# Hybrid decoder layer on one core: four more gate panels computed as block-product pairs ahead of the attention, four fewer threaded through it

## The chip, the cores and the metric

The kernel runs on one core of one Trainium2 chip. The metric is the device time of one execution in microseconds; the median of three runs is compared. The profile is of a fourth execution.

## The reference

One decoder layer on 512 tokens of width 2048, all in float32. Cut to what matters here:

```python
h = rmsnorm(x, norm_mix_g)                      # 512 x 2048
proj = h @ w_in                                 # q, six k/v streams, branch gates, u, v, merge gates
q, kv, nsa_g, u, v, merge_g = split(proj)       # merge_g: 2 x 2048 columns
kc, vc = compress_blocks(kv[0]), compress_blocks(kv[1])
o_a = nsa_attention(q, kc, vc, kv[2], kv[3], kv[4], kv[5], sigmoid(nsa_g))
o_b = spatial_gating(gelu(u), gelu(v), ...)
g = sigmoid(merge_g)                            # 512 x 2 x 2048
merged = g[0] * (o_a @ w_proj_a) + g[1] * (o_b @ w_proj_b)
x = x + merged @ w_mix_out
x = x + cross_attention(rmsnorm(x), rmsnorm(mem))
x = x + (silu(gt) * up) @ w_ffn_out             # gt, up = rmsnorm(x) @ w_ffn_in
out = rmsnorm(x)
```

The attention has 16 heads in 4 groups of keys, dimension 64, and for each query three softmaxes: over 31 compressed tokens, over selected blocks of 64 (all eight of them are selected here, so this one is plain causal attention) and over a window of 512.

## The kernel before

**Products.** Every float32 operand is split into a high and a low part; a product of 128 x 128 weights with 512 tokens is three TensorE matmuls of 512 columns (high with high, high with low, low with high; lines 987 to 989). The program calls the weight block with its three matmuls a *tile*. A *panel* is 128 output columns of a projection: 16 tiles, whose weights come in four *quarters*. For each quarter ScalarE casts the raw weights to the high part (`high`, line 2210) and VectorE subtracts to get the low part (`low`, line 1519, or both in `split`, lines 1498 and 1500). These two operations are called a split below.

**Block-product pairs.** Two panels can instead be made as a *pair*: the product of the 2 x 2 blocks (two weight halves by two halves of the inner dimension and of the tokens) by seven instead of eight block products, each a `half_unit` (lines 1078 to 1090) of 8 steps with 512 + 256 columns each. `G_TILES` lists which panels are made so: keys and values to compress, values, queries, and ten of the merge gates. Each pair costs ScalarE seven casts of 128 x 1024 and three evacuations, VectorE seven subtractions and some sums, SP three loads, GpSimd one adding DMA, and ScalarE two stores to HBM (`g_store`). Three buffers for the split weights are used in turn (`wg_hi`, `wg_lo`, unit number modulo 3); two of the three share their memory with the split buffers of plain panels (`w_hi`, `w_lo`).

**The order of stages** before the attention: memory keys and values; six plain merge-gate panels ("m0", `PLAIN_GATES`); the pairs (`G_PAIRS` of them); two key projections, value rows, the compression; then the attention; then the spatial gate ("sv", "su"), and the projections "ab", where all 32 gate panels are read back from HBM.

**The attention** is written out by hand as a list of *steps*, run by all engines in their own order. Its work is 32 *halves* (numbers `hu` 0 to 31): for each of four query chunks `qi` of 128 queries (first chunk to fourth chunk: 128, 256, 384, 512 keys), four key groups, and two pairs of heads. A half takes two score steps in the first chunk, four in the second and third, five in the fourth. Per step:

- TensorE (`scores`, line 1188) makes scores; VectorE (line 1714) masks them and takes maxima; ScalarE (line 2427) makes exponentials and their sums.
- After the last score step of a half, s, VectorE makes coefficients (1 over the sums, times the branch gate; lines 1726 and 1730) in step s+1, right after the maxima of that step. GpSimd scales the half's probabilities by them: first the compressed block for both heads (line 2798), then four blocks of 128 queries by 128 to 512 keys (line 2803).
- TensorE turns (transposes) the scaled probabilities: in step s+2 the compressed ones (line 1201), from step s+3 on the others, two 128-key blocks of both heads per step (line 1204). In the first chunk the first such turning needs all four of GpSimd's blocks, in the others two. ScalarE and VectorE split the result (lines 2445, 1742), and two steps after the turning TensorE weighs the values with it (`weigh`, lines 1215, 1219; `LAG = 2`). The last turning of a half falls into the first score step of the next or the one after, and in all but the first chunk the turning in step s is one of the half before.

```python
if part == 0 and 0 < hu <= len(HALVES):        # VectorE, in step s + 1, after low_max(step)
    dve.wait_ge(exp_done, step)
    dve.reciprocal(coef[:, ub], den[:, ub])
```

**What is threaded through it.** The merge-gate panels that are neither plain nor in pairs are computed between the attention's own matmuls. `spread` (line 170) deals their tiles to the 129 steps so that each step gets about the same TensorE cost, by `step_cost`; in a step, TensorE takes a third of the tiles ahead of the scores, a third ahead of the turning, and the rest ahead of the weighing. Where a step ends a quarter, ScalarE and VectorE split a later one at the end of that step, three quarters ahead, VectorE after its other work and so before the maxima of the next step; where it ends a panel, ScalarE evacuates and stores the gates (`gates_out`, line 2290).

```python
for step in range(STEPS):                      # TensorE
    tiles = TILES_AT[step]
    third = (len(tiles) + 2) // 3
    gate_tiles(tiles[:third])
    ...
    scores(step)
    gate_tiles(tiles[third:2 * third])
    ...
    turn_probs(*TURN_AT[step])
    gate_tiles(tiles[2 * third:])
```

## Time and profile before

| what | us |
|---|---|
| median of 3 runs | 2755.34 (2754.51 to 2755.74) |
| the profiled execution | 2756.18 |
| its span, first to last instruction | 2754.4 |
| its mean granted TensorE clock | 0.998 |
| stage of the 13 pairs | 143.2 to 398.5 |
| attention, first scores to first row of the spatial gate | 472.0 to 792.9 |

The profile is one execution of the program. The engines are PE (TensorE's matmuls), PEld (its weight loads, which overlap the matmuls), DVE (VectorE), ACT (ScalarE), POOL (GpSimd) and SP. L12 is line 12 of the kernel. A time in brackets behind a row is how long the engine was idle before it, and what ended that. A matmul's end is modelled, so distances are read from start to start.

### The profile page before, as it was taken

Reading aid. Unit: us, or ns where it says so; the run is one execution under the profiler, and the core shown is the slowest. Engines: PE = TensorE matmul, PEld = TensorE weight load, DVE = VectorE, ACT = ScalarE, POOL = GpSimd, SP = SyncE. Lnnn points to the kernel's source line nnn. Section 1 sums busy time; section 2 is a strip of 40 time slices with the busy share of each in tenths; the row PEclk is TensorE's granted clock in tenths of the full one; section 3 lists DMA queues with packets and bytes.
Section 4 is the critical chain, followed back from the end, with each engine's and each line's share of the span. In section 5 each row is a group of like instructions: output and inputs, shape, how many; then the busy total and the mean of one; then the engine's idle time right before and its main releaser. Section 6 shows DMA issues by size and latency. Waiting matters only on the chain.

```text
span 2754.4 us, 38103 instructions
## 1 busy us (share of the span) xinstructions
PE 2713.5 (99%) x14221; PEld 2301.5 (84%) x14221; DVE 2105.2 (76%) x2998; ACT 1209.7 (44%) x1923; POOL 450.5 (16%) x418
## 2 busy tenths in 40 slices
PE   8999999999999999999999999999999999999997
PEld 7888888888888888888877888888888888888886
DVE  6777874667755555555687899999999998988887
ACT  6344432766631222211144555555555555443334
POOL 0000002545520545411000000000000000010000
PEclk9999999999999999999999999999999999999999
DMA  8488866332233455444345788888888888999982
GB/s 243 131 188 181 199 157 165 81 92 66 58 96 99 105 141 152 137 115 114 92 137 142 165 214 205 218 204 210 204 214 211 210 206 250 301 305 297 302 263 92
DMA packets 648106, 479.38 MB, mean 174 GB/s; under 512 B 14612, under 2 KB 589448, under 8 KB 642056
## 3 DMA queue, kind: packets, MB, share of 16 engines
q1 hardware_dynamic: 568048, 416.58, 51.6%
q0 software_dynamic: 58896, 36.70, 10.2%
q10 hardware_dynamic: 21000, 23.92, 2.7%
q8 instruction: 103, 1.69, 0.3%
q14 instruction: 59, 0.48, 0.1%
HBM read 413.98 MB, written 63.18 MB: 173 GB/s over the span
## 4 chain that ended last, share of the span: by engine, by line
PE 89%; DVE 5%; ACT 3%; issue 2%; POOL 1%; DMA 1%; DVEq 0%; ACTq 0%; SPq 0%
PE banks L987 10%; PE banks L988 10%; PE banks L989 10%; PE banks L1419 10%; PE banks L1416 9%; PE banks L1417 9%; PE banks L1481 4%; PE banks L1483 4%; PE banks L1482 4%; PE banks L1085 3%; PE banks L1088 3%; PE banks L1086 3%; PE banks L1188 1%; PE banks L1204 1%; PE banks L1247 1%
## 5 line engine op out<-in xcount | busy, mean ns | idle before, releaser
L987 PE MATMUL banks<-act_hl,w_hi 128*128 128x512 f32 (+1 forms) x816 | 325.8, 399 | 2.4 <-DVE w_lo L1519 2.4
L1498 DVE CAST w_hi<-raw 128x512 fp32r<-128x512 f32 (+1 forms) x232 | 139.8, 603 | 245.0 <-PE banks L989 166.7
L988 PE MATMUL banks<-act_hl,w_hi 128*128 128x512 f32 (+1 forms) x816 | 319.7, 392 | 0.0
L989 PE MATMUL banks<-act_hl,w_lo 128*128 128x512 f32 (+1 forms) x816 | 319.5, 392 | 0.0
L1417 PEld LDWEIGHTS banks<-t_hl,wf_lo 128*128 128x128 f32 x1312 | 246.5, 188 | 58.3
L1419 PE MATMUL banks<-t_hl,wf_hi 128*128 128x512 f32 x656 | 259.4, 396 | 0.0
L1416 PE MATMUL banks<-t_hl,wf_hi 128*128 128x512 f32 x656 | 259.2, 395 | 0.0
L1417 PE MATMUL banks<-t_hl,wf_lo 128*128 128x256 f32 x1312 | 257.7, 278 | 0.0
L1951 DVE TENSOR_TENSOR wf_lo<-raw_f,wf_hi 128x1024 fp32r<-128x1024 f32 x164 | 200.4, 1222 | 56.7 <-ACT wf_hi L2599 56.7
L2599 ACT ACTIVATE wf_hi<-raw_f 128x1024 fp32r<-128x1024 f32 x164 | 173.8, 1060 | 136.9 <-PE banks L1419 83.6
L1417 PEld LDWEIGHTS banks<-tok_hl,wf_lo 128*128 128x128 f32 x984 | 184.8, 188 | 43.7
L1481 PE MATMUL banks<-wo_hi,h_full 128*128 128x512 f32 x560 | 218.9, 391 | 0.8 <-DVE wo_lo L1985 0.8
L1483 PE MATMUL banks<-wo_lo,h_full 128*128 128x512 f32 x560 | 218.0, 389 | 0.0
L1482 PE MATMUL banks<-wo_hi,h_full 128*128 128x512 f32 x560 | 217.9, 389 | 0.0
L1419 PE MATMUL banks<-tok_hl,wf_hi 128*128 128x512 f32 x492 | 194.6, 396 | 0.0
L1416 PE MATMUL banks<-tok_hl,wf_hi 128*128 128x512 f32 x492 | 194.4, 395 | 0.0
L1417 PE MATMUL banks<-tok_hl,wf_lo 128*128 128x256 f32 x984 | 193.3, 278 | 0.0
L2599 ACT ACTIVATE wf_hi<-s 128x1024 fp32r<-128x1024 f32 x123 | 130.2, 1059 | 137.9 <-PE banks L1419 137.9
L1500 DVE TENSOR_TENSOR w_lo<-raw,w_hi 128x512 fp32r<-128x512 f32 (+1 forms) x232 | 180.8, 779 | 8.0
L989 PEld LDWEIGHTS banks<-act_hl,w_lo 128*128 128x128 f32 (+1 forms) x816 | 152.5, 187 | 34.4
L2889 POOL DMA_DIRECT2D s<-in_w_ffn_in_dram x40 | 62.1, 1554 | 705.6 <-DMA s<-in_w_ffn_in_dram 705.6
L987 PEld LDWEIGHTS banks<-act_hl,w_hi 128*128 128x128 f32 (+1 forms) x816 | 152.8, 187 | 28.1 <-issue 3.0
(357 smaller groups left out, 6568.8 us busy)
## 6 DMA issues: line engine op xcount, KB each, us to landing
raw_f<-in_w_ffn_in_dram SPq DMA_DIRECT2D x82, 1024.0 KB, 9.0
raw<-in_w_in_dram SPq DMA_DIRECT2D x42, 1024.0 KB, 5.6
h_full<-hidden_blocks SPq DMA_DIRECT2D x35, 1024.0 KB, 8.1
wo_raw<-in_w_ffn_out_dram SPq DMA_DIRECT2D x32, 1024.0 KB, 10.0
raw_g<-in_w_in_dram SPq DMA_DIRECT2D x26, 1024.0 KB, 8.8
hidden_blocks<-tok_hl SPq DMA_DIRECT2D x44, 512.0 KB, 6.1
s<-in_w_ffn_in_dram SPq DMA_DIRECT2D x40, 512.0 KB, 6.2
s<-in_w_ffn_in_dram POOLq DMA_DIRECT2D x40, 512.0 KB, 6.5
```

Source lines behind the costliest of these rows:

```text
L987: pe.matmul(dst, w_hi[:, q, j, 0:m], hi, start=first, stop=False)
L988: pe.matmul(dst, w_hi[:, q, j, 0:m], lo, start=False, stop=False)
L989: return pe.matmul(dst, w_lo[:, q, j, 0:m], hi, start=False, stop=last)
L1416: pe.matmul(dst, w_h[:, k], both(k), start=start and k == 0, stop=False, skip_group_check=True)
L1417: mm = pe.matmul(dst[:, 0], w_l[:, k], both(k)[:, 0], start=False, stop=False, skip_group_check=True)
L1419: mm = pe.matmul(dst, w_h[:, k], both(k), start=False, stop=last, skip_group_check=True)
L1481: pe.matmul(dst, hi, wo_hi[g % 3][:, k], start=STARTS[j] and q == 0 and k == 0, stop=False, skip_group_check=True)
L1482: pe.matmul(dst, lo, wo_hi[g % 3][:, k], start=False, stop=False, skip_group_check=True)
L1483: mm = pe.matmul(dst, hi, wo_lo[g % 3][:, k], start=False, stop=last, skip_group_check=True)
L1500: dve.tensor_tensor(w_lo[:, q, :, 0:width], src, w_hi[:, q, :, 0:width].bitcast(F32), ALU.subtract).then_inc(split_done, 1)
L1951: dve.tensor_tensor(wf_lo[g % 3][:].rearrange("p k n -> p (k n)"), src, wf_hi[g % 3][:].rearrange("p k n -> p (k n)").bitcast(F32), ALU.su ...
L2599: act.activation(wf_hi[g % 3][:].rearrange("p k n -> p (k n)"), src, ACT.Copy).then_inc(f_hi, 1)
```

## The change

Four merge-gate panels (numbers 16 to 19) go from the attention to the list of pairs: 15 pairs in place of 13, 12 threaded panels (192 tiles) in place of 16 (256 tiles). The number of half units becomes 105 in place of 91, and the last one falls on another of the three buffers; the first two entries of the two buffer lists are exchanged for that, and with them a wait in ScalarE's order: the cast for unit 0 now writes where the last plain gate panel's first two quarters lie, and comes after the wait for them. The `LAG` of two steps between turning and weighing is the same in both.

```diff
--- before.py
+++ after.py
@@ -38,9 +38,9 @@
 PAIRS = FK - PLAIN
 HK, HT = DK // 2, T // 2
 PLAIN_GATES = 6
-G_TILES = [("c", n) for n in range(0, 4, 2)] + [("v", n) for n in range(0, 4, 2)] + [("q", n) for n in range(0, 8, 2)] + [("merge", n) for n in range(PLAIN_GATES, PLAIN_GATES + 10, 2)]
+G_TILES = [("c", n) for n in range(0, 4, 2)] + [("v", n) for n in range(0, 4, 2)] + [("q", n) for n in range(0, 8, 2)] + [("merge", n) for n in range(PLAIN_GATES, PLAIN_GATES + 14, 2)]
 G_PAIRS = len(G_TILES)
-GATES_AHEAD = PLAIN_GATES + 10
+GATES_AHEAD = PLAIN_GATES + 14
 OUT_H = (2, 4, 4, 4, 4, 4)
 OUT_M0 = (0, 2, 6, 10, 14, 18)
 OUT_RUNS = [(c, b) for c in range(len(OUT_H)) for b in range(2)]
@@ -58,7 +58,7 @@
 
 
 
-assert G_PAIRS % 2 == 1 and (7 * G_PAIRS - 1) % 3 == 0
+assert G_PAIRS % 2 == 1 and (7 * G_PAIRS - 1) % 3 == 2
 assert 2 * sum(OUT_H) == FK and PAIRS % 2 == 1 and T // 64 <= 16 and T <= 512
 
 
@@ -256,8 +256,8 @@
 
         gate_m0 = at("gate_m0", [P, 2, T], F32, C + 32 * KIB)
         raw_g = [at("raw_g0", [P, 2, 2, HK * P], F32, C), at("raw_g1", [P, 2, 2, HK * P], F32, base)]
-        wg_hi = [at(f"wg_hi{i}", [P, HK, P], F32R, o) for i, o in enumerate((C + 24 * KIB, base + 16 * KIB, base + 20 * KIB))]
-        wg_lo = [at(f"wg_lo{i}", [P, HK, P], F32R, o) for i, o in enumerate((C + 28 * KIB, base + 24 * KIB, base + 28 * KIB))]
+        wg_hi = [at(f"wg_hi{i}", [P, HK, P], F32R, o) for i, o in enumerate((base + 16 * KIB, C + 24 * KIB, base + 20 * KIB))]
+        wg_lo = [at(f"wg_lo{i}", [P, HK, P], F32R, o) for i, o in enumerate((base + 24 * KIB, C + 28 * KIB, base + 28 * KIB))]
         n_hl = [at(f"n_hl{k}", [P, 2, 4 * HT], F32R, B + 8 * k * KIB) for k in range(HK)]
         n_hi, n_lo = ([n_hl[k][:, w].rearrange("p (a t) -> p a t", t=HT) for k in range(HK)] for w in range(2))
         n_sum = [at(f"n_sum{k}", [P, 4, HT], F32, B + (8 * k + 4) * KIB) for k in range(HK)]
@@ -2314,8 +2314,8 @@
                     row_sums_high(k - 1)
                 if q == 1:
                     gates_out(ph, n - 1, n - 1, gate_m0)
+            act.wait_ge(quarters_done, ph.end() - 2)
             g_unit_high(0)
-            act.wait_ge(quarters_done, ph.end() - 2)
             g_unit_high(1)
             gates_out(ph, ph.n - 1, ph.n - 1, gate_m0)
             def g_store(p):
```

`spread` deals the 192 tiles anew over all 129 steps, so the tiles move in every part of the attention. Three places, each as the engine's list has it, before and with the change. In the names, prob and prob_c are the probabilities that GpSimd scales, act_hl is the split normalised input and w_hi, w_lo the split gate weights, so three rows L987, L988, L989 are one gate tile.

TensorE, half 29 (fourth chunk), from the turning of the compressed probabilities to the first turning of the others, before:

```order
L1201 MATMUL banks<-ident,prob_c 32x128 x2
L1219 MATMUL banks<-prob_t_111,v_hl 128x256 x4
L987 MATMUL banks<-act_hl,w_hi 128x512
L988 MATMUL banks<-act_hl,w_hi 128x512
L989 MATMUL banks<-act_hl,w_lo 128x512
L1188 MATMUL banks<-k_sel,q_hl 128x512 x2
L1204 MATMUL banks<-ident,prob 128x128 x4
```

and with the change:

```order
L1201 MATMUL banks<-ident,prob_c 32x128 x2
L1219 MATMUL banks<-prob_t_109,v_hl 128x256 x4
L1188 MATMUL banks<-k_sel,q_hl 128x512 x2
L1204 MATMUL banks<-ident,prob 128x128 x4
L1219 MATMUL banks<-prob_t_110,v_hl 128x256 x4
```

One tile that stood between the two turnings is gone from there.

TensorE, half 21 (third chunk), from the turning in the first score step after s to the turning of the compressed probabilities, before:

```order
L1204 MATMUL banks<-ident,prob 128x128 x4
L1219 MATMUL banks<-prob_t_109,v_hl 128x256 x4
L987 MATMUL banks<-act_hl,w_hi 128x512
L988 MATMUL banks<-act_hl,w_hi 128x512
L989 MATMUL banks<-act_hl,w_lo 128x512
L1188 MATMUL banks<-k_sel,q_hl 128x416 x2
L987 MATMUL banks<-act_hl,w_hi 128x512
L988 MATMUL banks<-act_hl,w_hi 128x512
L989 MATMUL banks<-act_hl,w_lo 128x512
L1201 MATMUL banks<-ident,prob_c 32x128 x2
```

and with the change:

```order
L1204 MATMUL banks<-ident,prob 128x128 x4
L1219 MATMUL banks<-prob_t_109,v_hl 128x256 x4
L987 MATMUL banks<-act_hl,w_hi 128x512
L988 MATMUL banks<-act_hl,w_hi 128x512
L989 MATMUL banks<-act_hl,w_lo 128x512
L1188 MATMUL banks<-k_sel,q_hl 128x416 x2
L1201 MATMUL banks<-ident,prob_c 32x128 x2
```

One of two tiles is gone here; a second one is gone ahead of the first of these turnings.

VectorE, half 21, from the split of the turned probabilities in step s to the coefficients in step s+1, before:

```order
L1742 TENSOR_TENSOR prob_t_110<-banks,prob_t_110 128x512
L1749 TENSOR_TENSOR oa<-banks,o_low 64x128 x2
L1519 TENSOR_TENSOR w_lo<-raw,w_hi 128x512
L1714 ISA banks,attn_max<-banks,cmp_mask 128x32
L1714 ISA attn_max 128x1
L1714 ISA banks,attn_max<-banks,causal 128x384
L1714 ISA attn_max 128x1
L1726 RECIPROCAL coef<-den 128x6
```

and with the change:

```order
L1742 TENSOR_TENSOR prob_t_110<-banks,prob_t_110 128x512
L1749 TENSOR_TENSOR oa<-banks,o_low 64x128 x2
L1714 ISA banks,attn_max<-banks,cmp_mask 128x32
L1714 ISA attn_max 128x1
L1714 ISA banks,attn_max<-banks,causal 128x384
L1714 ISA attn_max 128x1
L1726 RECIPROCAL coef<-den 128x6
```

The low part of a gate quarter (L1519) is gone from the end of this step; it stands in another.

## Rows read from the trace of the kernel before

**Rows 1.** The page, first part: busy time, share of the span, instructions.

```profile
PE 2713.5 (99%) x14221; PEld 2301.5 (84%) x14221; DVE 2105.2 (76%) x2998; ACT 1209.7 (44%) x1923; POOL 450.5 (16%) x418
```

**Rows 2.** Stretches: pairs, attention. Length, busy by engine, clock, DMA share, GB/s.

```profile
143.20:398.50 255.30, 254.38 (x1459) 221.52 (x1458) 199.89 (x206) 116.30 (x131) 18.68 (x12) 1.00 0.77 176
...
472.00:792.90 320.90, 315.48 (x1827) 265.48 (x1826) 215.45 (x719) 213.66 (x641) 161.60 (x193) 1.00 0.27 74
```

**Rows 3.** Waits of the attention: waiter, releaser, total us, times, longest.

```profile
POOL prob_c L2798 <- DVE coef L1730: 144.5, 32, 7.1
...
PEld banks L1204 <- POOL prob L2803: 9.5, 20, 1.0
...
PE banks L1204 <- POOL prob L2803: 2.9, 5, 0.8
```

**Rows 4.** Chain that ended last, plain panel: third matmul of 14 successive tiles.

```profile
460.30 0.24 PE banks L989
...
469.49 0.24 PE banks L989
```

**Rows 5.** Groups of instructions in the attention: count, busy us, mean ns, idle before.

```profile
L1519 DVE TENSOR_TENSOR w_lo<-raw,w_hi 128x512 fp32r<-128x512 f32 x63 | 45.9, 729 | 50.7 <-ACT w_hi L2210 50.2
L2210 ACT ACTIVATE w_hi<-raw 128x512 fp32r<-128x512 f32 x63 | 39.2, 623 | 0.0
```

**Rows 6.** Chain that ended last, start of the pairs: a cast, a subtraction.

```profile
147.57 1.07 ACT wg_hi L2307
148.66 1.24 DVE wg_lo L1599
```

**Rows 7.** Timeline, half 29: turning at s, GpSimd's scaling, first needed turning.

```profile
745.71 0.60 PE L1204 MATMUL banks<-ident,prob 128*128 128x128 f32 x4
...
748.60 0.70 POOL L2798 TENSOR_SCALAR prob_c<-prob_c,coef 128x32 f32<-128x32 f32 x2 [5.21 <-DVE coef L1730]
749.27 6.20 POOL L2803 TENSOR_SCALAR prob<-prob,coef 128x512 f32<-128x512 f32 x4
...
752.44 0.66 PE L1204 MATMUL banks<-ident,prob 128*128 128x128 f32 x4
```

**Rows 8.** Timeline, the same of halves 19 and 21.

```profile
631.75 0.60 PE L1204 MATMUL banks<-ident,prob 128*128 128x128 f32 x4
...
635.30 0.70 POOL L2798 TENSOR_SCALAR prob_c<-prob_c,coef 128x32 f32<-128x32 f32 x2 [4.12 <-DVE coef L1730]
...
638.49 0.66 PE L1204 MATMUL banks<-ident,prob 128*128 128x128 f32 x4
...
651.33 0.60 PE L1204 MATMUL banks<-ident,prob 128*128 128x128 f32 x4
...
655.53 0.70 POOL L2798 TENSOR_SCALAR prob_c<-prob_c,coef 128x32 f32<-128x32 f32 x2 [4.76 <-DVE coef L1730]
...
658.72 0.66 PE L1204 MATMUL banks<-ident,prob 128*128 128x128 f32 x4 [0.54 <-POOL prob L2803]
```

**Rows 9.** Chain that ended last, inside half 21's interval.

```profile
653.82 0.69 DVE w_lo L1519
```

**Rows 10.** Timeline, half 13: turning at s, GpSimd's blocks, first needed turning.

```profile
571.66 0.60 PE L1204 MATMUL banks<-ident,prob 128*128 128x128 f32 x4
...
576.33 3.70 POOL L2803 TENSOR_SCALAR prob<-prob,coef 128x256 f32<-128x256 f32 x4
...
578.91 0.60 PE L1204 MATMUL banks<-ident,prob 128*128 128x128 f32 x4
```

**Rows 11.** Timeline, half 3: GpSimd's blocks, weight load of the needed turning.

```profile
497.34 2.35 POOL L2803 TENSOR_SCALAR prob<-prob,coef 128x128 f32<-128x128 f32 x4
...
499.74 0.31 PEld L1204 LDWEIGHTS banks<-ident,prob 128*128 128x128 f32 x3 [0.52 <-POOL prob L2803]
```

**Rows 12.** Timeline, half 27: turning at s, first needed turning.

```profile
720.87 0.60 PE L1204 MATMUL banks<-ident,prob 128*128 128x128 f32 x4
...
728.29 0.66 PE L1204 MATMUL banks<-ident,prob 128*128 128x128 f32 x4
```

## The prediction

> **What bounds the kernel now.** I read the page's first part, then a table of stretches, then the waits of the attention, then its timeline half by half. The page has TensorE busy 99% of the span [rows 1]. The stretches show where that share is an average: the stage of 13 block-product pairs (143.2 to 398.5 us) has VectorE at 78% and GpSimd nearly empty, the attention stretch (472.0 to 792.9 us) has 320.9 us with TensorE at 315.5, VectorE at 215, ScalarE at 214 and GpSimd at 162 us [rows 2]. So both stages look bound by TensorE. The waits of the attention say how close the second one is to something else: TensorE's matmuls wait 2.9 us in 5 places for GpSimd's scaled probabilities (L2803), its weight loads 9.5 us in 20 places for the same line; GpSimd itself waits 144.5 us in 32 places, once per half, for VectorE's coefficients [rows 3]. That is the sign of a chain that is only just covered, once in each of 32 halves. What covers it is the gate work between its ends, and this is what the change takes out.
>
> **The two prices.** A gate tile (three 512-column matmuls) takes 0.707 us: 13 tiles lie between the two starts 460.30 and 469.49 [rows 4]. A whole panel of 16 tiles is 11.3 us. A pair of block products gives two panels in 254.4 us / 13 = 19.6 us [rows 2].
>
> **What the change adds and removes.** Four panels leave the attention: 64 x 0.707 = 45.2 us of TensorE work. Two more pairs come ahead of it: 2 x 19.6 = 39.1 us. On TensorE alone: **6.1 us less**. In the pair stage VectorE is busy 15.4 us of each 19.6 and ScalarE 8.9, and the DMA share is 0.77 [rows 2], in a steady rhythm, so two more pairs should cost what the 13 cost, their loads, stores and GpSimd's adding DMAs included. In the attention 16 splits leave ScalarE (0.62 us each, L2210) and VectorE (0.73 us each, L1519), four gate evacuations and stores leave ScalarE, and SP has four panel loads less [rows 5]; none of these engines ends the stage by its sum, but the splits matter below.
>
> **The swapped buffers and the moved wait.** The first unit's weights now go to the place that the last plain gate panel's first two quarters hold, so ScalarE's first cast waits until TensorE has two quarters left. Those are 24 matmuls, 8 x 0.707 = 5.7 us. Behind the wait stand one cast (1.07 us) and one VectorE subtraction (1.24 us) before unit 0 can start [rows 6], 2.3 us, so I cost it at nothing; the second cast stands where it stood. Uncovered it would cost at most 2.3 us. The third unit goes on waiting for the last gate store, as now.
>
> **The chain in each half.** Call s the last score step of a half. TensorE turns probabilities of the half before in step s; ScalarE copies them out, VectorE subtracts, adds the closed half, sometimes splits a weight quarter, takes the maxima of step s+1, and only then makes the coefficients; GpSimd scales the small block and then two (for the first query chunk four) probability blocks; only then can TensorE turn them, in step s+3. I call the time from the turning in s to the one in s+3 the interval. It cannot be shorter than the chain, and not shorter than TensorE's own work in it.
> - Fourth chunk (512 keys, half 29): turning 745.71, GpSimd starts 748.60, first needed turning 752.44, an interval of 6.73 us with 2.89 + 3.84, the latter being 0.67 plus half of 6.20 [rows 7]. Four tiles lie in it, and TensorE stands there as soon as GpSimd is done: the cover is just used up. Half 30 reads the same, 28 too.
> - Third chunk (384 keys): half 19 has no split at s: 3.55 + 3.19 = 6.74 us, no matmul waits; half 21 has one: 4.20 + 3.19 = 7.39 us, and TensorE has waited 0.54 us there [rows 8]. In the chain of half 21 the split's 0.69 us stands right ahead of the maxima [rows 9]. Five tiles lie in each.
> - Second chunk (256 keys, half 13): interval 7.25 us with 7 tiles and no wait; GpSimd starts its four blocks at 576.33 and has the two that are needed ready 1.85 us later, at 578.2; TensorE comes at 578.91 [rows 10]: 0.7 us to spare with a split in the chain, and more in halves without one.
> - First chunk (128 keys, half 3): GpSimd ends at 497.34 + 2.35 = 499.69 and TensorE's weight load starts at 499.74, having waited 0.52 us [rows 11]. Nothing to spare in most halves.
>
> **The sum.** The order now places fewer tiles in each interval. The planner gives, before and after, counted in the listed order:
> - fourth chunk: 6,5,5,5,4,4,4,6 tiles become 4,3,3,3,3,3,3,5. The four last halves lose one tile each with nothing to spare: 4 x 0.7 = 2.8 us of new waiting. The first four lose two (1.4 us), but their chain, 7.42 us in half 27 [rows 12] with ScalarE and VectorE busier there, may fall towards 6.7; I take 1.0 us each. Together 6.8 us.
> - third chunk: TensorE's own work is 6.7 us with 5 tiles, so 3.2 without any. The counts 7,5,5,5,5,5,5,5 become 4,3,4,4,3,3,3,3: work of 6.0 us in three halves and 5.3 in five. The chain is 6.74 us, or 7.4 where a split stays at s (halves 17, 20 and 23). Waiting: 3 x 2.1 + 3 x 0.75 + 2 x 1.45 = 11.5 us, against 5 x 0.7 in the halves that have a split at s now and about 1 us in the three others, 4.5 us. Together 7.0 us more.
> - second chunk: mostly two tiles less (1.4 us) against 0.7 us or more to spare, and splits that move to other halves: 2.5 us.
> - first chunk: one tile less per half, 8 x 0.7 = 5.7 us at most, its intervals overlap; I take about half, 2.5 us.
>
> New waiting 18.8 us, saved work 6.1 us: **+12.7 us**. The profiled execution took 2756.2 us (span 2754.4); that makes 2768.9 in its terms, and the median of the runs is 0.8 us lower: **2768 us**.
>
> Bounds: if every tile taken from the third and fourth chunk's intervals is lost (27 x 0.707 = 19.1 us), all of the first chunk's (5.7) and 5 us of the second's, the change costs 29.8 - 6.1 = 24 us. If the chains shorten all the way, because VectorE and ScalarE have a quarter fewer splits, and only the four last halves and those without a split wait, some 6 us come against 6.1 saved: no change.
>
> **A rule weighed against this.** The stretch table has TensorE busy 98% of the attention, more than any other engine [rows 2]. The Trainium skill (Perfetto Trace Analysis, Identifying the Most-Contended Engine) says the engine with the highest occupancy is the one to optimise first; by that rule alone the result would be 6.1 us less. The busy row agrees with it, the 20 waits do not. The same page (Optimization Strategy) says that a kernel with stretches of different contended engines may gain from interleaving them; that rule speaks against moving gate work out of the attention, and by it the result is above the old time, as in my sum.
>
> **The rivals.**
> - *TensorE stays the bound* (the chains shorten as fast as the work): 2755.3 - 6.1 = 2749 us. For it: TensorE's matmuls wait for GpSimd only 2.9 us of 320.9 now [rows 3], and VectorE has a third of the stretch free. Against it: the 20 waits of the weight loads, and half 29, whose chain holds no split that could leave it.
> - *Cover and saving cancel*: new waiting of 1 to 11 us, 2750 to 2760 us. For it: the spare time of the second chunk and the shorter queue ahead of each coefficient.
> - *The attention is bound by the other engines throughout*: it keeps its 320.9 us, and the two pairs come on top: 2755.3 + 39.1 = 2794 us. Against it: the little waiting now, and the second chunk's time to spare.
> - *The clock*: granted TensorE clock is 1.00 (2.4 GHz) in the attention in spite of its waits [rows 2]; longer waits could lower it. I give this no price, 1 in 50 inside the upper cases.
>
> **The numbers.** A measurement of this kernel tells about 0.2% (5.5 us) from no change: faster is below 2749.8, slower above 2760.8. My forecast, 2761 to 2778 us, has 0.74; cancelling 0.16; TensorE still the bound 0.06; wholly bound by others, or above 2778 for another reason, 0.04. The range leaves out the fastest case and the last one: 2753 to 2778 us.
>
> **What would show it.** Right: the pair stage 39 us longer; the attention stretch about 26 us shorter, not 45; TensorE waiting for L2803 in most of 32 places, for a total near 20 us; in half 29 three tiles and an interval still of 6.7 us; granted clock 1.00. Wrong: an interval that shrinks with its tiles (the chain then had spare time in the queues of ScalarE and VectorE), or waits that name L1519, L2290 or a DMA in place of GpSimd, or a pair that costs other than 19.6 us.

## The result and the profile after

The changed kernel takes 2779.8 us (median of four runs, 2778.81 to 2780.18), the kernel before 2755.54 us (2754.51 to 2756.91) beside it: a ratio of 1.0087 with a 95% interval of 1.0070 to 1.0105. It is **24.3 us slower**. The prediction was 2768 us, 2753 to 2778 us: the right side, about half the size, and the result lies 1.8 us above the range. The profiled execution took 2779.68 us, its span 2778.0 us.

The first part of the page, to be read beside [rows 1]:

```profile
PE 2711.4 (98%) x14253; PEld 2297.3 (83%) x14253; DVE 2124.0 (76%) x3014; ACT 1215.7 (44%) x1923; POOL 453.8 (16%) x420
```

TensorE does 2.1 us less work in a span that is 23.6 us longer. The whole loss is idle time on the engine that was taken to be the bound. The page does not say where; the stretches do. Pairs and attention of the changed kernel (length, busy time by engine, clock, DMA share, GB/s), to be read beside [rows 2]:

```profile
141.60:435.50 293.90, 293.02 (x1681) 255.24 (x1680) 230.75 (x238) 134.31 (x151) 21.76 (x14) 1.00 0.78 177
510.40:815.20 304.80, 274.88 (x1633) 228.20 (x1631) 203.79 (x702) 200.86 (x621) 160.49 (x193) 1.00 0.22 60
```

With the ends taken at the same instructions in both kernels (start of the first to start of the last matmul of the pairs, first score of the attention to the first row of the spatial gate; the rows above begin up to 0.5 us earlier):

| us | before | after | difference | predicted |
|---|---|---|---|---|
| pairs | 254.8 | 293.7 | +38.9 | +39.1 |
| attention | 320.4 | 304.7 | -15.7 | -26.4 |
| all the rest | 2179.2 | 2179.5 | +0.3 | 0 |

The pairs cost what 2 x 19.6 us said. The rest moves between 2178.5 and 2182.5 us over all the kernels of this study, so its 0.3 us is not the change's. What is left is the attention: 45.2 us of tiles left it and it became only 15.7 us shorter, so **29.5 us of new waiting** came, where 18.8 us were forecast. In the changed kernel TensorE is busy 274.9 of 304.8 us there, against 315.5 of 320.9 us before.

The waits of the attention, changed kernel (waiter, releaser, total us, times, longest), to be read beside [rows 3]:

```profile
POOL prob_c L2798 <- DVE coef L1730: 132.0, 32, 6.1
...
PEld banks L1204 <- POOL prob L2803: 27.0, 27, 2.2
PEld banks L1201 <- POOL prob_c L2798: 19.3, 24, 1.9
PE banks L1204 <- POOL prob L2803: 18.7, 22, 1.7
...
PE banks L1201 <- POOL prob_c L2798: 10.3, 13, 1.6
```

L2803 makes TensorE's matmuls wait in 22 places for 18.7 us, nearly the predicted "total near 20 us", though not "in most of 32 places". But a second line stands beside it: the turning of the small block (L1201) waits for GpSimd's scaling of that block (L2798) for 10.3 us in 13 places, where it had waited 0.7 us in 2 places. GpSimd scales that block first, as soon as it has the coefficients. A wait there says that the coefficients themselves are late, not that GpSimd is slow. The prediction had only L2803 in view. The same row in the kernel before:

```profile
PE banks L1201 <- POOL prob_c L2798: 0.7, 2, 0.6
```

By query chunk (128, 256, 384 and 512 keys, eight halves each). Windows of the kernel before:

```profile
472.00:519.90 47.90, 46.59 (x275) 38.62 (x274) 31.55 (x158) 37.23 (x143) 26.09 (x49) 1.00 0.25 67
519.90:598.30 78.40, 77.80 (x444) 66.40 (x443) 51.44 (x185) 51.81 (x164) 34.34 (x48) 1.00 0.36 96
598.30:679.10 80.80, 78.40 (x454) 65.63 (x452) 57.18 (x181) 55.21 (x160) 43.41 (x48) 1.00 0.29 78
679.10:776.60 97.50, 97.07 (x573) 81.76 (x573) 68.99 (x185) 63.08 (x164) 54.77 (x49) 1.00 0.19 55
```

and of the changed kernel:

```profile
510.40:555.40 45.00, 40.01 (x246) 33.29 (x244) 31.12 (x160) 35.06 (x140) 25.94 (x49) 1.00 0.24 65
555.40:629.10 73.70, 68.32 (x395) 57.09 (x396) 48.34 (x179) 49.34 (x159) 33.48 (x47) 1.00 0.31 83
629.10:706.00 76.90, 68.29 (x405) 56.37 (x403) 54.32 (x177) 52.01 (x154) 43.42 (x49) 1.00 0.21 55
706.00:800.90 94.90, 84.66 (x512) 70.02 (x512) 64.39 (x180) 59.13 (x158) 54.59 (x49) 1.00 0.14 42
```

Tiles taken out of each (counted in the order) at 0.707 us, less what the chunk shrank by (measured from the first score at 472.5 and 510.5 us), is its new waiting:

| chunk | tiles out | their work | shrank by | new waiting | predicted |
|---|---|---|---|---|---|
| first | 9 | 6.4 | 2.5 | 3.9 | 2.5 |
| second | 16 | 11.3 | 4.7 | 6.6 | 2.5 |
| third | 16 | 11.3 | 3.8 | 7.5 | 7.0 |
| fourth | 20 | 14.1 | 2.6 | 11.5 | 6.8 |

(The last three tiles lie behind the fourth chunk and waited 0.1 us.) The third chunk is right, the fourth and the second carry the miss: 4.7 and 4.1 us of 10.7.

### The profile page after: what moved, and what is told of

Same layout as the page of the kernel before. It is cut to its first block, busy times and chain, and to the rows that moved or that the text cites. A ratio compares the mean times of both kernels' runs of the same rounds, so it can differ in the third digit from the quotient of the medians.

```text
span 2778.0 us, 38195 instructions
## 1 busy us (share of the span) xinstructions
PE 2711.4 (98%) x14253; PEld 2297.3 (83%) x14253; DVE 2124.0 (76%) x3014; ACT 1215.7 (44%) x1923; POOL 453.8 (16%) x420
## 4 chain that ended last, share of the span: by engine, by line
PE 81%; DVE 7%; POOL 4%; ACT 3%; issue 2%; DMA 2%; ACTq 0%; DVEq 0%; POOLq 0%; SPq 0%
PE banks L1419 9%; PE banks L1416 9%; PE banks L1417 9%; PE banks L987 8%; PE banks L989 8%; PE banks L988 8%; PE banks L1481 4%; PE banks L1482 4%; PE banks L1483 4%; PE banks L1085 3%; PE banks L1088 3%; PE banks L1086 3%; POOL prob L2803 2%; DVE w_lo L1519 1%; PE banks L1247 1%
## 5 line engine op out<-in xcount | busy, mean ns | idle before, releaser
L987 PE MATMUL banks<-act_hl,w_hi 128*128 128x512 f32 (+1 forms) x752 | 299.4, 398 | 3.0 <-DVE w_lo L1519 2.4
L989 PE MATMUL banks<-act_hl,w_lo 128*128 128x512 f32 (+1 forms) x752 | 293.8, 391 | 0.0
L988 PE MATMUL banks<-act_hl,w_hi 128*128 128x512 f32 (+1 forms) x752 | 293.8, 391 | 0.0
L989 PEld LDWEIGHTS banks<-act_hl,w_lo 128*128 128x128 f32 (+1 forms) x752 | 140.1, 186 | 31.6
L987 PEld LDWEIGHTS banks<-act_hl,w_hi 128*128 128x128 f32 (+1 forms) x752 | 140.4, 187 | 27.0 <-issue 3.6
## 6 DMA issues: line engine op xcount, KB each, us to landing
wo_raw<-in_w_ffn_out_dram SPq DMA_DIRECT2D x32, 1024.0 KB, 10.5
```

What stands on the lines that cost most here:

```text
L987: pe.matmul(dst, w_hi[:, q, j, 0:m], hi, start=first, stop=False)
L988: pe.matmul(dst, w_hi[:, q, j, 0:m], lo, start=False, stop=False)
L989: return pe.matmul(dst, w_lo[:, q, j, 0:m], hi, start=False, stop=last)
```

## What the longer chain consists of

Half 28, in the fourth chunk, with the changed kernel. TensorE's timeline (start, busy us, line; the bracket is idle time ahead of it):

```profile
757.26 0.60 PE L1204 MATMUL banks<-ident,prob 128*128 128x128 f32 x4
...
758.16 0.60 PE L1204 MATMUL banks<-ident,prob 128*128 128x128 f32 x4
...
766.27 0.44 PE L1204 MATMUL banks<-ident,prob 128*128 128x128 f32 x2 [1.72 <-POOL prob L2803]
```

The turning in step s is the one at 758.16, the first needed one in step s+3 the one at 766.27: an interval of 8.11 us, where the prediction had 6.7 us. There is another turning, that of step s-1, at 757.26, only 0.90 us ahead of it. No gate tile stands between the two any more; in half 29 of the kernel before two of them and a score stood there, and the two turnings lay 2.29 us apart.

The chain that ended last goes through that earlier turning (start, length, engine, line). In this view a matmul begins where the one before it is let go, so its starts lie a little behind those of the timeline:

```profile
757.42 0.45 PE banks L1204 x4
...
757.89 0.61 ACT prob_t L2445
...
758.52 0.69 DVE prob_t L1742
759.22 0.19 DVE oa L1749
...
759.44 0.28 DVE oa L1749
...
759.75 0.69 DVE w_lo L1519
760.45 0.61 DVE banks L1714
...
761.11 0.55 DVE prob_t L1742
761.66 0.10 DVE banks L1714
...
761.97 0.19 DVE coef L1726
...
762.18 0.17 DVE coef L1730
...
762.44 0.70 POOL prob_c L2798 x2
763.14 3.09 POOL prob L2803 x2
```

From 758.52 to 762.35 us VectorE is in the chain without a break. It works off one step (subtraction L1742 for the turning of s-1, two closing adds L1749, the gate split L1519), the maxima L1714 of step s, the subtraction for the turning of s, the maxima of s+1, and then the coefficients. The turning in s is late for none of it: its own result is only wanted at 761.11 us. **In this half the chain starts at the turning in s-1**, and from there to GpSimd's start it is 762.44 - 757.26 = 5.18 us.

The same distance stood in the trace of before, in a row that the prediction did not ask for. TensorE's timeline of the kernel before, the turning in s-1 of half 29:

```profile
743.42 0.60 PE L1204 MATMUL banks<-ident,prob 128*128 128x128 f32 x4
```

GpSimd starts at 748.60 [rows 7]: 5.18 us again. In the halves 26 to 31 of the kernel before it is 5.18 or 5.19 us every time, while the distance from the turning in s is 3.58 us in two of them and 2.89 or 2.90 in four. All measured in the two timelines, in us:

| half | before: s-1 to GpSimd | s to GpSimd | after: s-1 to GpSimd | s to GpSimd |
|---|---|---|---|---|
| 26 | 5.18 | 3.58 | 5.64 | 4.04 |
| 27 | 5.19 | 3.59 | 5.86 | 4.27 |
| 28 | 5.18 | 2.89 | 5.18 | 4.28 |
| 29 | 5.18 | 2.89 | 4.51 | 2.92 |
| 30 | 5.18 | 2.90 | 5.19 | 3.60 |
| 31 | 5.18 | 2.89 | 5.01 | 3.41 |

In the changed kernel neither distance is constant. Halves 24, 28 and 30 have 5.18 or 5.19 us with a split in step s-1, and half 29 has 4.51 us without one. In halves 26, 27 and 31 the chain that ended last also passes through ScalarE's queue: its exponentials, in half 27 the cast of a split behind them, and in half 26 the evacuation of a gate panel, which stands ahead of the copy of the turning in s:

```profile
734.71 0.50 ACT gate_out L2290
```

So it is the queues of VectorE and ScalarE from step s-1 on that make the coefficients late, and only in the fourth chunk. In the third, the turning in s-1 lies 2.4 to 3.0 us ahead of that in s, and in half 21 the chain that ended last begins at the turning in s, in both kernels. There it is the distance from s that repeats, as predicted: 3.55 us in halves 19 and 20 before and 18, 21 and 22 after, all without a split in step s, and 4.20 or 4.21 us with one in halves 17, 21 and 22 before and 20 after.

From GpSimd's start to the first needed turning it is 3.83 us in all the halves of the table. That makes a loop in the fourth chunk of the kernel before: from one first needed turning, 3.06 us of TensorE's own work to the turning in s-1, 5.18 us to GpSimd's start, 3.83 us to the next first needed turning, 12.07 us in all. The kernel before starts GpSimd every 12.06 to 12.08 us from half 25 to half 31. In the changed kernel the seven steps from half 24 to half 31 (714.26 to 797.10 us) take 11.83 us each on the mean, in spite of two or three tiles (1.4 to 2.1 us) less per half: only the 3.06 us can shrink (to 2.36 us where a tile is gone there), and what stands between s-1 and s+3 is ScalarE's, VectorE's and GpSimd's.

## The experiments

Each row is a time in the same measurement as the kernel before; where a row names no number of runs it is a single one, good to about 2 us (the runs of the kernel before in these measurements gave 2754.5 to 2758.3 us). Gains over the changed kernel are taken from its 2779.8 us.

| kernel | us | before beside it | attention |
|---|---|---|---|
| e1: before, wait moved alone | 2756.6 | 2756.4 | 320.2 |
| e2: before, twelve panels threaded, 13 pairs | 2741.9 | 2756.4 | 305.6 |
| e3: after, coefficients before maxima | 2776.2 | 2756.4 | 300.7 |
| e4: before, the same | 2754.8 | 2756.4 | 319.7 |
| e5: after, gate splits a step later | 2766.9 | 2757.0 | 292.1 |
| e6: after, everything late | 2766.9 | 2757.0 | 288.9 |
| e7: after, other places for the tiles | 2773.3 | 2757.0 | 297.7 |
| e8: before, everything late | 2751.5 | 2757.0 | 315.9 |
| e9: after, GpSimd in smaller pieces | 2777.3 | 2756.0 | 301.2 |
| e10: after, combined | 2753.4 (10 runs) | 2756.0 | 278.2 |
| e11: before, combined | 2746.5 (5 runs) | 2756.0 | 310.5 |
| e12: after, combined, other places | 2750.1 (10 runs) | 2755.3 | 275.5 |

The column on the attention is the steadiest measure, since the stages outside it and the pairs, whose code is the same, add up to 2178.5 to 2182.5 us.

### e1: the moved wait alone

```diff
-            g_unit_high(0)
             act.wait_ge(quarters_done, ph.end() - 2)
+            g_unit_high(0)
             g_unit_high(1)
```

> The kernel before, with ScalarE's wait for the last plain panel's quarters moved ahead of the first unit's cast, and nothing else. If the moved wait is covered: 2755.5 us, within 1 us, the first unit starting as before. If it is a part of the loss: up to 2.3 us more (2757.8).

2756.57 us against 2756.38 us. The chain that ended last at the start of the pairs, to be read beside [rows 6]:

```profile
146.86 1.07 ACT wg_hi L2307
...
147.96 1.24 DVE wg_lo L1599
```

The cast and the subtraction stand in the chain as they did before, and the wait cost nothing. The pair stage, the other edit outside the attention, is measured above as +38.9 us.

### e2: twelve panels threaded, without the pairs

This kernel leaves out the four panels that the change moves: they are not computed, and one DMA fills their rows from the input.

```diff
-GATES_AHEAD = PLAIN_GATES + 10
+GATES_AHEAD = PLAIN_GATES + 14
```

> The kernel before with 12 threaded gate panels in place of 16 and still 13 pairs; four gate panels are not computed (their rows are filled from x by one DMA in the attention). If the whole loss beyond the pairs' price lies in the attention's own waits: the attention stretch falls from 320.9 to about 305 us as with the full change, and the time is 2755.5 - 16 = 2739.5 us (2738 to 2742). If some of the loss comes from the two added pairs or from the swapped buffers, the attention shrinks by more than 20 us and the time is below 2736.

2741.92 us, and the stretch of the attention (columns as above):

```profile
472.70:778.30 305.60, 276.11 (x1630) 229.53 (x1629) 203.83 (x702) 200.77 (x621) 160.23 (x193) 0.99 0.23 64
```

305.6 us, as in the changed kernel (304.7); the second to fourth chunk are each within 0.1 us of its, and the first is 1.0 us longer. So the lost time belongs to the attention with twelve panels in it. It is not brought on by what the two pairs leave behind, their DMAs or their buffers. Against the kernel before beside it e2 gains 14.5 us, where the changed kernel loses 24.3: 38.8 us for the two pairs.

### e3 and e4: coefficients ahead of the maxima

The first theory, which took the chain from the turning in s: VectorE's coefficients stand behind the maxima of step s+1, so put them first. e3 is the changed kernel, e4 the one before.

```diff
             for step in range(STEPS):
                 hu, part = STEP_OF[step] if step < ITEMS else (len(HALVES), step - ITEMS)
-                if step < ITEMS:
-                    low_max(step)
                 if part == 0 and 0 < hu <= len(HALVES):
...
                     dve.tensor_tensor(coef[:, ub], coef[:, ub], gates[:, qi, j * 12 + 6 * pr:j * 12 + 6 * pr + 6], ALU.mult).then_inc(coef_done, 1)
+                if step < ITEMS:
+                    low_max(step)
```

> The changed kernel, with VectorE making the coefficients of a closed half ahead of the maxima of step s+1 in place of behind them. Theory A (the chain runs through VectorE's queue, and the maxima of step s+1 and TensorE's scores stand in it for nothing): GpSimd starts 0.5 to 1.1 us sooner in most of the 32 halves, TensorE's waiting for GpSimd falls from 29 to 5 to 12 us, the time to 2757 to 2764 us. Rival B (the coefficients wait for the exponentials of step s anyway, or GpSimd's own blocks bound it): under 5 us gained, 2775 to 2780. Rival C (the later maxima delay the exponentials by as much): no gain, or slower.

> The kernel before with the same exchange on VectorE. Theory A: TensorE's matmuls wait only 3.6 us for GpSimd in it, its weight loads some more; 2 to 4 us gained, 2751.5 to 2753.5. Rivals B and C: 2755.5 or more.

e3 gave 2776.15 us, a gain of 3.6 us where 16 us or more were expected: a miss, inside what rival B gave. e4 gave 1.6 us where 2 to 4 were expected, which a single run does not tell from nothing; its attention is 0.7 us shorter. Waits of the attention in e3:

```profile
PE banks L1204 <- POOL prob L2803: 16.0, 20, 1.7
...
PE banks L1201 <- POOL prob_c L2798: 5.5, 9, 1.1
```

and VectorE's timeline in half 28 of e3:

```profile
758.75 0.19 DVE L1724 RECIPROCAL coef<-den 128x6 f32<-128x6 f32 x1 [0.30 <-ACT prob L2427]
```

The coefficients now wait for ScalarE's exponentials of step s, and those wait for VectorE's maxima of s, which stand behind the gate split and the closing adds of the step before. In the third chunk the distance from the turning in s to GpSimd fell (halves 21 and 22: 3.55 to 2.98 us). In the fourth it did not: half 28 has 5.19 us from s-1 and 4.29 us from s, as without the edit. By chunk the attention changed by +0.2, -1.0, -2.8 and -0.4 us: a gain in the third, where the chain starts at s, and next to none in the fourth. There, what held the coefficients up was not what stands behind the turning in s, and this run turned the theory to s-1.

### e5: the gate splits one step later

If VectorE's queue from s-1 on is the chain, then taking a gate split out of it must shorten it, wherever the turning in s lies. The edit runs the splits of a step after the next step's maxima and coefficients. Nothing is left out. A split of step s thus goes behind the coefficients, but one of step s-1 only goes behind the maxima of s, and stays ahead of them.

```diff
+                if step:
+                    gate_lows(step - 1)
                 short = len(SCORES[min(hu, len(HALVES) - 1)]) == 2
...
-                for k in QUARTERS_AT[step]:
-                    k += AHEAD
...
+            gate_lows(STEPS - 1)
```

> The changed kernel, with VectorE's part of each gate split (L1519) moved from the end of its step to behind the maxima and coefficients of the next. Theory A2 (VectorE's queue from the turning in step s-1 to the coefficients is the chain; a split in it costs 0.7 us, and one stands in it in about half of the 32 halves, at step s-1 or s): 8 to 12 us gained, 2768 to 2772 us, and half 28's time from the turning in s to GpSimd falls from 4.3 to about 3.6 us. Rival D (GpSimd and ScalarE hold the chain, VectorE only follows): under 3 us gained.

2766.91 us, 12.9 us less than the changed kernel and 1.1 us below what was expected of the s-1 theory. The attention lost 12.6 us. From s-1 to GpSimd's start it is 4.48 to 5.01 us in the fourth chunk, where it was 4.51 to 5.86.

One expectation was missed, and it tells most: in half 28 the distance from the turning in s was to fall to 3.6 us and came out at 4.11. Its split is one of step s-1, and it is still in the chain that ended last, now between the maxima of s and the subtraction for the turning in s:

```profile
747.84 0.60 DVE w_lo L1519
...
749.37 0.04 DVE coef L1734
```

From s-1 that half has 5.01 us, only 0.17 less than before the edit; halves 24 and 30, whose splits also belong to step s-1, gained as little. By chunk e5 shortened the attention by 2.9, 5.8, 1.1 and 2.9 us. By the order 15 of the 32 halves of the changed kernel have a split in step s, 5, 6, 3 and 1 by chunk, and at 0.7 us each that is about 10.5 us (an estimate). So e5 shows what the splits of step s cost, but it does not tell a chain that starts in s-1 from one that starts in s: both ask for this gain. What tells them apart is the trace of the fourth chunk. TensorE's waits of the attention in e5:

```profile
PE banks L1204 <- POOL prob L2807: 15.4, 21, 1.7
...
PE banks L1201 <- POOL prob_c L2802: 3.7, 7, 1.0
```

### e6 and e8: splits, closing adds and maxima all behind the coefficients

```diff
+                if step < ITEMS:
+                    low_max(step)
+                if step:
+                    gate_lows(step - 1)
+                    closed(step - 1)
...
-                if step - 1 in CLOSE_AT:
-                    own = CLOSE_AT[step - 1]
...
+            closed(STEPS - 1)
```

> As the run before it, and also the closing adds (L1749, 0.59 us, once per half, in the chain of the second to fourth chunk) behind the maxima of the next step and the coefficients ahead of the maxima of step s+1. Theory A2: the three together take 0.6 us in 24 halves and what the single exchange gave (3.6 us) on top, 2752 to 2762 us in all. Rival D: no more than the sum of what the single ones give, 2770 or more.

> The kernel before with the three VectorE moves (split late, closing adds late, coefficients first). Its matmuls wait 3.6 us for GpSimd: theory A2 gives 2 to 3.5 us gained, 2752 to 2754 us; if the late splits or adds hold something else up, slower than 2755.5.

e8, on the kernel before, gave 2751.48 us, 5.5 us faster, a little more than expected; its attention is 4.5 us shorter. e6, on the changed kernel, gave 2766.87 us, no better than e5: a miss by 5 us. TensorE's waits of the attention in e6:

```profile
PE banks L1204 <- POOL prob L2810: 8.7, 15, 1.6
...
PE banks L1215 <- DVE oa L1732: 7.0, 6, 1.7
```

The matmuls' waits for GpSimd fell from 19.1 us in e5 (both lines) to 8.7, and a new one took part of the place: TensorE cannot begin the values of a new half (L1215) before the closing adds have read its accumulator bank. 5.8 of the 7.0 us lie in the first chunk (510 to 557 us), where a half has only two steps, so that a closing add one step later is late at once. e8 pays it too, at 4.1 us in 6 places. There it is 3.8 us in the first chunk, and it is nearly all the matmul waiting that e8 has left, so it was the next thing to take out of both kernels (e10 and e11). e6's attention is 3.2 us shorter than e5's; its stages outside are 3.2 us longer, so the totals agree. Some of e6's first chunk was also the clock: from 544.9 to 548.6 us, where TensorE had waited for these adds, the granted clock was 0.50 (1.2 GHz).

### e7: more tiles between the turnings

The change's own count of tiles, placed otherwise: the first two steps behind the end of each half of the second to fourth chunk, s+1 and s+2, are counted as cheaper and so get more tiles, the others fewer. In the second to fourth chunk 18 more tiles than in the change lie between the turnings in s and s+3.

```diff
-        TILES_AT = spread(GATE_TILES, [step_cost(step) for step in range(STEPS)])
+        EARLY = {STEP0[hu + 1] + d for hu in range(len(HALVES)) if HALVES[hu][2] for d in range(2)}
+        TILES_AT = spread(GATE_TILES, [step_cost(step) - 1400 * (step in EARLY) for step in range(STEPS)])
```

> The changed kernel with the same 192 tiles dealt so that steps s+1 and s+2 of each half of the second to fourth chunk get more of them (their cost is counted 1400 lower), which puts about 17 tiles back between the turnings in s and s+3. Theory of my prediction (a chain of fixed length from the turning in s, covered by what lies in it): up to 17 x 0.707 = 12 us of waiting gone, 2768 to 2772 us. Theory A2: the steps s-1 and s then lie closer together, VectorE's work for both piles up ahead of the coefficients, and most of it is lost again: 2774 to 2780 us.

2773.32 us, 6.5 us less, and 7.1 us less in the attention. It lies between what the two theories gave, below the s-1 theory's interval and above the other's. TensorE's waits of the attention in e7:

```profile
PE banks L1205 <- POOL prob L2804: 16.7, 21, 1.3
...
PE banks L1202 <- POOL prob_c L2799: 3.6, 4, 1.4
```

So where the tiles stand is worth something too, about half of what e5's queue order is worth. The run does not tell which of the two effects of a moved tile did it: its own cover, or a split that moves with it. By the order only 8 halves have a split in step s now, against 15. And it understates the gain, since the first chunk lost tiles by it (25 in place of 31), and the clock fell there. Before 522 us TensorE idled 1.5 of 3 us; then the granted clock was 0.50 (1.2 GHz) for almost 7 us of nearly steady work:

```profile
523.00:529.00 6.00, 6.00 (x23) 4.93 (x21) 3.26 (x18) 2.55 (x13) 3.11 (x6) 0.53 0.07 17
```

The starts of successive gate matmuls lie 0.43 us apart in it and 0.23 us at full clock, so it cost some 3 us (an estimate). The first chunk is 1.1 us longer than the changed kernel's; the other three together are 6.8 us shorter.

### e9: GpSimd's first pieces smaller

The other link of the chain, from GpSimd's start to the first needed turning. In the third and fourth chunk GpSimd scales the two leading 128-column blocks of both heads first, then the rest.

```diff
+                n = (qi + 1) * P
+                pieces = [(1, 0, n), (2, 0, n)] if qi < 2 else [(1, 0, 2 * P), (1, 2 * P, n), (2, 0, n)]
+                for b, n0, n1, e in [p + (e,) for p in pieces for e in range(2)]:
+                    pr_rows = prob[:, hu % 2, 2 * (b - 1) + e, n0:n1]
```

> The changed kernel, with GpSimd scaling, in the third and fourth chunk, the first 256 columns of the two blocks first (two more and shorter operations per half), and TensorE's first turning waiting for those alone. VectorE's order is as in the change. If GpSimd's part is in the chain to its full length, the chain is 1.2 us shorter in 8 halves and 0.6 us in 8: up to 14.6 us gained, but the turning of the compressed block then waits as before, so 8 to 13: 2767 to 2772 us. If only VectorE's queue counts: under 4 us gained.

2777.32 us, 2.5 us less where 8 to 13 us were expected: a miss. The windows of the third and the fourth chunk in e9:

```profile
631.50:710.30 78.80, 69.05 (x405) 56.01 (x404) 54.27 (x176) 51.74 (x155) 47.54 (x63) 1.00 0.20 54
710.30:799.80 89.50, 84.44 (x514) 69.94 (x514) 64.28 (x180) 59.35 (x159) 60.00 (x66) 1.00 0.15 42
```

The fourth chunk is 5.4 us shorter than in the change, the third 1.9 us longer. Scaling in pieces costs GpSimd 4.1 us more in the third chunk (47.5 against 43.4 us) and 5.4 us in the fourth, for the same elements in 14 and 17 more listed operations, so about 0.3 us each. With 384 keys what is taken off the front is small (3.19 to 2.56 us from GpSimd's start to the first needed turning in half 21), and the next turnings, which need the last pieces, come later: from the turning in s-1 to that in s it is 3.61 us there, and was 2.95.

### e10 and e11: all of it together

e6 with the closing adds late only where the closed half is not in the first chunk, and e9's pieces. e10 is the changed kernel, e11 the one before.

```diff
+            def closed(step, late):
+                if step - 1 in CLOSE_AT and late == (HALVES[CLOSE_AT[step - 1]][2] > 0):
...
+                    closed(step - 1, True)
...
+                closed(step, False)
```

> The changed kernel with all: splits late, coefficients first, closing adds late except in the first chunk, GpSimd's first columns first. The waits left in the run with all three VectorE moves were 8.7 us for GpSimd and 7.0 us for the late closing adds in the first chunk. Both theories together: 2766.9 - 7 - 5 = 2755 us (2752 to 2759), the attention stretch 280 us or less, against the 275.7 that TensorE's own work would take.

> The kernel before with the same four moves. Its waits for GpSimd are gone already with three of them (2751.5 us, one look); 1 us of late closing adds comes back: 2750.5 us (2749.5 to 2752). If 15 pairs were the better count once the chain is short, the run with the change would have to be below this one; by the sums above it is not, since its cover is still thinner.

e10: 2753.38 us (2752.42 to 2755.07), a ratio to the kernel before of 0.9990 [0.9981, 1.0000], as expected. That is 26.4 us under the changed kernel, and its attention is 26.5 us shorter. e11: **2746.5 us** (2746.36 to 2747.49), a ratio of 0.9964 [0.9950, 0.9978], 4 us below the 2750.5 us expected and outside the 2749.5 to 2752 us given. In the first chunk e10 differs from e6, and e11 from e8, only by the place of the closing adds. It is 40.8 us long in e10 and 49.1 in e6, 44.3 in e11 and 49.3 in e8: the late adds had cost 8.4 and 5.0 us, the slower clock of e6 included. Attention of e10, and one of its waits:

```profile
510.90:789.10 278.20, 269.62 (x1630) 230.02 (x1629) 201.94 (x700) 197.49 (x621) 179.31 (x225) 1.00 0.24 66
```

```profile
PE banks L1205 <- POOL prob L2813: 7.8, 15, 0.9
```

and the same of e11, where the weight loads' wait is the only one left on TensorE for GpSimd:

```profile
472.90:783.40 310.50, 309.83 (x1823) 266.52 (x1821) 214.04 (x716) 208.00 (x641) 178.95 (x225) 1.00 0.28 76
```

```profile
PEld banks L1205 <- POOL prob L2813: 0.8, 3, 0.4
```

With sixteen panels threaded the chains are covered in every half, and TensorE is busy 309.8 of 310.5 us. With twelve they are still not, even after all four moves: TensorE waits in 15 places.

### e12: fifteen pairs at their best

e10 with the pieces only in the fourth chunk (e9's loss in the third avoided) and e7's places.

```diff
-        TILES_AT = spread(GATE_TILES, [step_cost(step) for step in range(STEPS)])
+        TILES_AT = spread(GATE_TILES, [step_cost(step) - 1400 * (step in EARLY) for step in range(STEPS)])
...
+                pieces = [(1, 0, n), (2, 0, n)] if qi < 3 else [(1, 0, 2 * P), (1, 2 * P, n), (2, 0, n)]
```

> The combined run of the changed kernel (2753.4 us, attention 278.2 us, 265.3 would be without any waiting), with two more: GpSimd's first columns first only in the fourth chunk, and 17 tiles dealt back between the turnings in s and s+3. In the change alone the same dealing gave 6.5 us, in spite of VectorE's queue. With the queue short, theory A2 and the theory of cover both ask for more: 4 to 8 us, 2745.5 to 2749.5 us. Below 2746.5 us (the kernel before with the four moves) 15 pairs would be the better count; I expect the two within 3 us of each other. If the bias only moves the waits: 2752 to 2754.

2750.14 us (2749.29 to 2753.06), a ratio of 0.9982 [0.9973, 0.9992]: faster than the kernel before, 0.6 us above what was expected, and 3.6 us slower than e11. TensorE's wait in e12:

```profile
PE banks L1206 <- POOL prob L2814: 5.2, 10, 1.2
```

The attention is 275.5 us, 35.0 us shorter than e11's, and the two pairs that pay for it cost 38.9 us. The sum is +3.9 us, near the 3.6 measured. **e11 is the version that beats both kernels**, by 9.5 us over the one before beside it (2756.0) and 33 us over the changed one.

## Why the prediction was right and where it failed

**The two prices, right.** The pairs cost 38.9 us where 39.1 were forecast. The tile's 0.707 us stands behind every row of the table by chunk.

**The moved wait, right.** Costed at nothing, and e1 alone shows 0.2 us, within a single run's spread.

**The sign and the kind of loss, right.** The gate tiles were cover for a chain through ScalarE, VectorE and GpSimd that comes once per half, and taking them out laid it bare. The waits name GpSimd's L2803, the attention shrank much less than its tiles, the clock stayed at 1.00. Half 29 has three tiles and an interval of 6.75 us, as predicted; from GpSimd's start to the needed turning it is 3.19 us in the third chunk and 3.83 us in the fourth, as in [rows 7, 8].

**The rule.** TensorE was the busiest engine of the attention, 98% of it. The Trainium skill (Perfetto Trace Analysis, Identifying the Most-Contended Engine) has the engine with the highest occupancy optimised first; taken as a forecast, as the prediction did, 6.1 us less of its work is 6.1 us gained, and measured was a loss of 24.3 us. For TensorE the same section of the Trainium skill goes by the busy share of the weight loads, which the prediction left out; it was 83% here (265.5 of 320.9 us) and shows more room, though not the chain. The Trainium skill's rule on interleaving stretches (the same page, Optimization Strategy) spoke against the change, and the runs agree: with the same four moves sixteen threaded panels (e11) are 7 us faster than twelve (e10).

**The step that failed: "the chain in each half".** It said "TensorE turns probabilities of the half before in step s; ScalarE copies them out, VectorE subtracts ..., and only then makes the coefficients", so it put the chain's start at the turning in s. With that, the interval of a half can only keep its length or shrink when tiles leave. In the third chunk that start is right. In the fourth, the coefficients hang on what VectorE and ScalarE have queued since the turning in s-1. Where tiles between s-1 and s went away, the turning in s came earlier, the coefficients did not, and the interval from s grew: 6.73 to 8.11 us in half 28, and 7.42 to 8.10 us in half 27, of which the text said that it "may fall towards 6.7". Twenty tiles left the fourth chunk and only 2.6 us came back. The prediction counted one lost tile each for the last four halves and 1.0 us for the first four, 6.8 us; it measured 11.5 us. The earlier start is shown by the chains that ended last and by the distance of 5.18 us, not by an experiment of its own; e3 agrees with it, since taking the maxima of s+1 from behind the turning in s gave 2.8 us in the third chunk and 0.4 in the fourth.

**The term of the second chunk, mis-sized.** "0.7 us or more to spare, and splits that move to other halves: 2.5 us"; it measured 6.6 us. The spare time was read in half 13 alone. By the order a gate split stood in step s of four of the eight halves before (9, 12, 13, 15) and stands in six now (8 to 11, 14, 15), though there are fewer splits in all; from the turning in s to GpSimd's start it is 3.83 to 4.77 us in halves 9, 10, 11, 14 and 15. These five hold 4.4 of the chunk's 5.4 us of waiting for L2798, half 15 alone 1.61 us; half 13 holds the rest. None of it is waiting for L2803, on which the spare time had been counted.

**The first chunk**, 3.9 us for 2.5, was taken as half of 5.7 us, and **the third**, 7.5 us for 7.0, had its chains read half by half, with the split at s told from its absence. It is the one that was right.

**The bound was right, the choice within it was not.** If every tile taken from the bounded intervals is lost the text had 29.8 us of waiting and +24 us; measured were 29.5 and +24.3. The range ended at 2778 us because anything above was given 0.04 together with the rival of a wholly bound attention. The text itself had written "nothing to spare" against the four last halves and most of the first chunk, and a chain with no slack gives back little of what is taken out of its cover; the upper bound deserved the larger chance.

**How much was waiting before?** The text read 2.9 us of matmul waits. e11 does the same TensorE work in 310.5 us with next to no wait, so the kernel before lost 320.4 - 310.5 = 9.9 us in the attention. By that measure the chain was not "only just covered", it was already 10 us short, and after the change 304.7 - (310.5 - 45.2) = 39.4 us.

**What stays open.** In e7 the cover of the moved tiles and the split that moves with them were not told apart. No run takes the splits of step s-1 alone from ahead of the coefficients, so what the start in s-1 is worth was not measured by itself. Smaller pieces for the first and second chunk were not tried.

## What to carry to other kernels

Before filler work is taken from between the ends of a chain on other engines, follow that chain back on the engine whose queue is in order until a distance stays the same from one repetition to the next (here 5.18 us in six halves of the fourth chunk, from a step earlier than assumed), and do so for each form of the repetition: in the third chunk the start was where it had been assumed. A chain without slack in most repetitions returns little of the removed work (2.6 of 14.1 us in the fourth chunk), so price it at the upper bound. And look at what stands in the in-order queue ahead of the critical result: moving independent work of 0.7 us one step later was worth more (12.9 us here, and 9.5 us together with its companions in the kernel before) than the 6.1 us of TensorE work that the exchange was to save.

## What the runs showed beyond that

- **Busy time of TensorE hides waiting.** From the first score on, the kernel before shows 315.0 us busy in the attention and e11 309.8 us, with the same matmuls (some 1825 recorded in each). About 5 us of "busy" were then waiting inside matmuls whose ends are modelled; no view shows it directly. The matmuls' wait rows name 3.6 us for GpSimd and the weight loads' 13.1 us, where 9.9 us were lost; in the changed kernel they name 29.0 and 46.3 us, where 39.4 us were lost. The loss lies between the two rows, and the prediction took the lower one alone.
- **The clock stayed up in the change, but not in every run.** The granted clock is 1.00 (2.4 GHz) in all four chunks of the changed kernel, with TensorE idle up to 10.2 us of 94.9. In the first chunk of three other kernels it was 0.50 (1.2 GHz) for a while, each time behind waits of TensorE: almost 7 us in e7, and 3 to 4 us in e6 (from 544.9 us) and in e2 (from 493.6 us), whose first chunk is the 1.0 us longer one. The prediction gave longer waits that lower the clock 1 in 50; in the change it did not happen.
- **GpSimd's scaling has a fixed part**: about 0.3 us for each further operation at the same number of elements (e9), and its groups say the same by size. In the third chunk of e9 (line, engine, operation, shape, count, busy us, mean ns of one):

```profile
L2805 POOL TENSOR_SCALAR prob<-prob,coef 128x384 f32<-128x384 f32 x14 | 17.7, 1274 | 0.0
L2805 POOL TENSOR_SCALAR prob<-prob,coef 128x256 f32<-128x256 f32 x18 | 17.2, 966 | 0.0
...
L2805 POOL TENSOR_SCALAR prob<-prob,coef 128x128 f32<-128x128 f32 x15 | 8.9, 606 | 0.0
```

606, 966 and 1274 ns for 128, 256 and 384 columns: about 0.33 us for each 128 columns and 0.28 us for the operation itself.
